# Values first by token tile in the first attention, and shared statistics for two norms in a row, in a two-stack transformer on one core

## The reference, cut to what matters

```
def first_block(x, ...):                       # layer 1 (second layer)
    k_blocks, v_blocks, k_mean = shared_kv(x, kv_norm, w_kv)   # rmsnorm(x, kv_norm) @ w_kv
    h = rmsnorm(x, norm_mixer[layer])
    q = (h @ w_q[j]).reshape(B, T, N_HEADS, HEAD_DIM)
    o = moba_attention(q, k_blocks, v_blocks, k_mean, rel_bias)
    x = x + o @ w_o[j]
    x = x + swiglu(rmsnorm(x, norm_ffn[layer]), w_gate_up[layer], w_down[layer])
    return rmsnorm(x, final_norm)              # = the second stack's x
rmsnorm(x, g) = x * rsqrt(mean(x*x) + 1e-6) * g
```

## Time and profile before

| | us |
|---|---|
| median of three runs | 1184.52 |
| profiled execution, its own time | 1182.94 |
| span of the profiled execution | 1180.9 |
| TensorE busy | 1142.3 (97%) |
| VectorE busy | 786.6 (67%) |
| ScalarE busy | 536.1 (45%) |
| GpSimd busy | 35.1 (3%) |

### The profile page before, as it was taken

The page is one execution under the profiler, slowest core; times in us unless marked ns, Lnnn a source line. Parts: engine busy times, 40 slices in busy tenths (PEclk is TensorE's granted clock), DMA queues, the critical chain, the costliest instruction groups (busy, mean ns, idle before and its releaser), DMA issues.

```text
span 1180.9 us, 17170 instructions
## 1 busy us (share of the span) xinstructions
PE 1142.3 (97%) x6750; PEld 992.2 (84%) x6750; DVE 786.6 (67%) x990; ACT 536.1 (45%) x696; POOL 35.1 (3%) x49
## 2 busy tenths in 40 slices
PE   6899999899999999998999999999999999999997
PEld 4788888799878888888988788888899887888886
DVE  4766666746667666666677676666766766766665
ACT  4534334446654334335566543343345665433432
POOL 0000000000000000001200000000030000000000
PEclk9899999999999999998999999999999999999999
DMA  9565656664337555575623375556763234665560
GB/s 286 186 213 183 206 181 201 195 210 140 114 115 231 187 191 194 197 214 155 198 76 105 116 236 187 191 191 199 214 179 117 94 108 143 198 194 181 183 205 36
DMA packets 167672, 205.14 MB, mean 174 GB/s; under 512 B 19983, under 2 KB 150535, under 8 KB 167618
## 3 DMA queue, kind: packets, MB, share of 16 engines
q1 hardware_dynamic: 167618, 204.40, 53.7%
HBM read 203.22 MB, written 1.16 MB: 173 GB/s over the span
## 4 chain that ended last, share of the span: by engine, by line
PE 91%; DVE 3%; SPq 2%; ACT 2%; issue 1%; POOL 1%; DMA 0%; DVEq 0%; POOLq 0%; ACTq 0%
PE bank L1296 27%; PE bank L1300 14%; PE bank L1270 13%; PE bank L1271 13%; PE bank L1272 13%; PE bank L1487 3%; PE bank L1499 2%; PE bank L1379 1%; ACT junk L626 1%; PE bank L1509 1%; POOL rstd L564 1%; PE bank L1701 1%; DVE xn L907 1%; DVE x L889 1%; PE bank L1644 1%
## 5 line engine op out<-in xcount | busy, mean ns | idle before, releaser
L615 ACT ACTIVATE whi<-raw 128x2048 fp32r<-128x2048 f32 x177 | 339.0, 1916 | 414.0 <-PE bank L1300 271.4
L879 DVE TENSOR_TENSOR wlo<-raw,whi 128x2048 fp32r<-128x2048 f32 x177 | 405.7, 2294 | 162.9 <-ACT whi L615 162.8
L1296 PE MATMUL bank<-h_both,whi 128*128 128x512 f32 x1376 | 327.6, 390 | 0.0
L1296 PEld LDWEIGHTS bank<-h_both,whi 128*128 128x128 f32 x1376 | 255.0, 188 | 50.8
L1300 PEld LDWEIGHTS bank<-h_both,wlo 128*128 128x128 f32 x1376 | 176.7, 191 | 6.9
L1300 PE MATMUL bank<-h_both,wlo 128*128 128x256 f32 x1376 | 178.8, 283 | 0.0
L1270 PE MATMUL bank<-whi,o_hi 128*128 128x512 f32 x448 | 176.0, 393 | 0.6 <-DVE o_lo L1088 0.6
L1271 PE MATMUL bank<-wlo,o_hi 128*128 128x512 f32 x448 | 174.9, 390 | 0.0
L1272 PE MATMUL bank<-whi,o_lo 128*128 128x512 f32 x448 | 174.4, 389 | 0.0
L1270 PEld LDWEIGHTS bank<-whi,o_hi 128*128 128x128 f32 x448 | 84.3, 188 | 18.4 <-issue 2.3
L1272 PEld LDWEIGHTS bank<-whi,o_lo 128*128 128x128 f32 x448 | 84.1, 188 | 18.0
(11 more groups left out here) (154 smaller groups left out, 1146.8 us busy)
## 6 DMA issues: line engine op xcount, KB each, us to landing
raw<-in_w_gate_up SPq DMA_DIRECT2D x44, 1024.0 KB, 5.0
raw<-in_w_down SPq DMA_DIRECT2D x44, 1024.0 KB, 4.8
raw<-in_w_gate SPq DMA_DIRECT2D x22, 1024.0 KB, 5.3
raw<-in_w_up SPq DMA_DIRECT2D x22, 1024.0 KB, 5.2
raw<-in_w_in SPq DMA_DIRECT2D x20, 1024.0 KB, 6.1
raw<-in_w_o SPq DMA_DIRECT2D x12, 1024.0 KB, 4.8
raw<-in_w_kv SPq DMA_DIRECT2D x8, 1024.0 KB, 5.5
raw<-in_w_q SPq DMA_DIRECT2D x4, 1024.0 KB, 5.8
```

Of the source, the lines that this page charges most:

```text
L615: act.activation(whi[:, s, :], raw[:, s, :], ACT.Copy).then_inc(hi_ready, 1)
L879: dve.tensor_tensor(wlo[:, s, :], raw[:, s, :], whi[:, s, :].bitcast(F32), ALU.subtract).then_inc(lo_ready, 1)
L1296: pe.matmul(bank[bk + jj][:, :], hi[:, kc, jj * P:(jj + 1) * P], h_both[:, kc, :, :].rearrange("p a t -> p (a t)"), start=(kc == 0), stop= ...
```

## The change

In the first attention, the norm for keys and values comes first (version 2, now into `h_hi` and `h_lo`), the one for queries second (version 3, into `o_hi` and `o_lo`). Unit 0 is the values of head group 0, token-major: `first_token_major` for tile 0, then the transposes of tile 1, then tile 1. Unit 1 is the keys of group 0, with the transposes of the query norm between its two passes. Units 2 to 5 are the query quarters, and unit 2 is the one that goes through `first_feature_major`. VectorE gets its own order for this norm (`kv_norm`), in which the low part of unit 1's weights is computed in two halves between the steps of the norm.

Between the stacks, ScalarE squares both `x` (into `ssq`) and `x` times the final norm's gain (into `usq`), which VectorE writes to `xn`. Both powers of a tile are taken in one GpSimd instruction over two columns. The mixers' input is the scaled `xn` times one scalar times the gain; the new residual `x` is formed afterwards (`residual_out`), that of tile 1 behind the split of unit 84.

```
 def moba_script():
-    s = [("q_norm",)]
...
-    s += unit(0) + [("kv_norm",)] + unit(1) + [("kv_h",)]
+    s = [("kv_h",), ("q_norm",)] + unit(0) + [("q_h",)] + unit(1)
...
         def moba_src(n):
-            if n < 4:
-                return k8(a["w_q"][0], 256 * n)
+            if n < 2:
+                return k8(a["w_kv"], 0 if n else D)
+            if n < 6:
+                return k8(a["w_q"][0], 256 * (n - 2))
...
 # GpSimd, between the stacks
             for t in range(TT):
-                for v in (4, 5):
-                    rsqrt_tile(v, t)
+                pool.wait_ge(msq_ready, tile_no(5, t) + 1)
+                pool.tensor_tensor(rstd[:, t:t + 7:6], msq[:, t:t + 7:6], neghalf[:, 0:2], ALU.pow).then_inc(rstd_ready, 2)
...
 # ScalarE, between the stacks
+                    for h in range(2):
+                        square_x(0, h)
+                        square_scaled(0, h)
+                    split(u0 + 1)
+                    square_x(1, 0)
+                    square_x(1, 1)
+                    h_out(6, 0, 0)
+                    h_out(6, 0, 1)
+                    square_scaled(1, 0)
+                    square_scaled(1, 1)
                     for h in range(2):
                         h_out(6, 1, h)
...
 # VectorE, first attention
+            def kv_norm():
+                add_residual(2, 0, 0)
+                add_residual(2, 0, 1)
+                mean_square(2, 0)
+                normalise(2, 0, 0)
+                normalise(2, 0, 1)
+                add_residual(2, 1, 0)
+                h_lo_out(2, 0, 0)
+                h_lo_out(2, 0, 1)
+                add_residual(2, 1, 1)
+                split_half(MOBA_U + 1, 0)
+                mean_square(2, 1)
+                normalise(2, 1, 0)
+                normalise(2, 1, 1)
+                split_half(MOBA_U + 1, 1)
+                h_lo_out(2, 1, 0)
+                h_lo_out(2, 1, 1)
...
 # VectorE, between the stacks (final_norm_1)
+                def scaled(t, h):
...
+                    dve.tensor_tensor(xn[:, t, cols], x[:, t, cols], gx[:, cols], ALU.mult).then_inc(scaled_ready, 1)
+                def mean_squares(t):
...
+                    dve.tensor_scalar(msq[:, t:t + 1], ssq[:, t, 0:1], ssq[:, t, 1:2], EPS, ALU.add, ALU.add).then_inc(msq_ready, 1)
...
+                    then_wait(dve.tensor_scalar(msq[:, 6 + t:7 + t], msq[:, t:t + 1], EPS, usq[:, t, 0:1], ALU.mult, ALU.add))
+                    dve.tensor_tensor(msq[:, 6 + t:7 + t], msq[:, 6 + t:7 + t], usq[:, t, 1:2], ALU.add).then_inc(msq_ready, 1)
...
+                for h in range(2):
+                    add_residual(4, 0, h)
+                    scaled(0, h)
+                mean_squares(0)
+                add_residual(4, 1, 0)
+                add_residual(4, 1, 1)
+                for h in range(2):
+                    mixer_input(0, h)
+                for h in range(2):
+                    scaled(1, h)
+                for h in range(2):
+                    h_lo_out(6, 0, h)
+                mean_squares(1)
+                residual_out(0, 0)
+                for h in range(2):
+                    mixer_input(1, h)
+                residual_out(0, 1)
                 for h in range(2):
                     h_lo_out(6, 1, h)
+                split(MIX_U[0] + 1)
+                for h in range(2):
+                    residual_out(1, h)
...
 # TensorE, first attention
+                    if n == 0:
+                        first_token_major(u, 4, 0, 2)
+                        transposes(2, 1)
+                        used(first_token_major(u, 4, 1, 2))
+                    elif n == 1:
+                        feature_major(u, 5, ALL, 0, H)
+                        for t in range(TT):
+                            transposes(3, t)
+                        used(feature_major(u, 5, ALL, 1, H))
+                    elif n == 2:
+                        pe.wait_ge(proj_out, 1)
+                        used(first_feature_major(u, 4, O, 3))
```

More of the change, by code:

```diff
@@ L734, in _ @@
                 k = ev[0]
[L735 removed]
+                if k == "kv_h":
                     norm(2, late_split=MOBA_U + 1)
[L737 removed]
+                elif k == "q_h":
                     norm(3, False)
@@ L768, in mix, with next_square, square_x, square_scaled @@
                 if l == 0:
[L769 to L778, removed]
+                    done = [16]
+                    def next_square(src, t, h, acc):
+                        act.wait_ge(squares, done[0])
+                        act.activation(junk[:, :], src[:, t, h * HALF:(h + 1) * HALF], ACT.Square, scale=1.0 / 32,
+                                       accum_out=acc[:, t, h:h + 1]).then_inc(squares, 1)
+                        done[0] += 1
+                    def square_x(t, h):
+                        act.wait_ge(x_ready, 12 + 2 * t + h + 1)
+                        if t == 0 and h == 0:
+                            act.wait_ge(msq_ready, tile_no(3, 1) + 1)
+                        next_square(x, t, h, ssq)
+                    def square_scaled(t, h):
+                        act.wait_ge(scaled_ready, 2 * t + h + 1)
+                        next_square(xn, t, h, usq)
+                    for h in range(2):
[8 more added lines that the diff above has]
+                    square_scaled(1, 1)
                     for h in range(2):
@@ L942, in norm, with split_half @@
                         h_lo_out(j, t, h)
+            def split_half(n, part):
+                s = slot_of(n)
+                cols = slice(part * UNIT // 2, (part + 1) * UNIT // 2)
+                if part == 0:
+                    dve.wait_ge(hi_ready, n + 1)
+                i = dve.tensor_tensor(wlo[:, s, cols], raw[:, s, cols], whi[:, s, cols].bitcast(F32), ALU.subtract)
+                if part:
+                    i.then_inc(lo_ready, 1)
+            def kv_norm():
[15 more added lines that the diff above has]
+                h_lo_out(2, 1, 1)
             def lambdas():
@@ L1116, in _ @@
                 k = ev[0]
[L1117 to L1120, removed]
+                if k == "kv_h":
+                    kv_norm()
+                elif k == "q_norm":
                     for t in range(TT):
@@ L1142, in final_norm_1 @@
             def final_norm_1():
[L1144 to L1155, removed]
+                gx, gz = gains[:, 1, :], gains[:, 0, :]
@@ new lines, in scaled @@
+                def scaled(t, h):
+                    cols = slice(h * HALF, (h + 1) * HALF)
+                    if (t, h) == (0, 0):
+                        dve.wait_ge(gains_in[1], 16 * 3)
+                        dve.wait_ge(xT_ready, 4 * (HT_NO[6] - 1))
+                    dve.wait_ge(x_ready, 12 + 2 * t + h + 1)
+                    dve.tensor_tensor(xn[:, t, cols], x[:, t, cols], gx[:, cols], ALU.mult).then_inc(scaled_ready, 1)
+                def mean_squares(t):
+                    dve.wait_ge(squares, 22 if t else 19)
+                    dve.wait_ge(rstd_ready, tile_no(4, t))
+                    dve.tensor_scalar(msq[:, t:t + 1], ssq[:, t, 0:1], ssq[:, t, 1:2], EPS, ALU.add, ALU.add).then_inc(msq_ready, 1)
+                    dve.wait_ge(msq_ready, tile_no(4, t) + 1)
+                    dve.wait_ge(squares, 16 + 4 * t + 4)
+                    then_wait(dve.tensor_scalar(msq[:, 6 + t:7 + t], msq[:, t:t + 1], EPS, usq[:, t, 0:1], ALU.mult, ALU.add))
+                    dve.tensor_tensor(msq[:, 6 + t:7 + t], msq[:, 6 + t:7 + t], usq[:, t, 1:2], ALU.add).then_inc(msq_ready, 1)
@@ new lines, in mixer_input, with residual_out @@
+                def mixer_input(t, h):
+                    cols = slice(h * HALF, (h + 1) * HALF)
+                    if (t, h) == (0, 0):
+                        dve.wait_ge(gains_in[0], 16 * 4)
+                    dve.wait_ge(rstd_ready, tile_no(5, t) + 1)
+                    dve.scalar_tensor_tensor(out=xn[:, t, cols], in0=xn[:, t, cols], scalar=rstd[:, 6 + t:7 + t],
+                                             in1=gz[:, cols], op0=ALU.mult, op1=ALU.mult).then_inc(xn_ready, 1)
+                def residual_out(t, h):
+                    cols = slice(h * HALF, (h + 1) * HALF)
+                    dve.scalar_tensor_tensor(out=x[:, t, cols], in0=x[:, t, cols], scalar=rstd[:, t:t + 1],
+                                             in1=gx[:, cols], op0=ALU.mult, op1=ALU.mult).then_inc(x_ready, 1)
@@ L1165, in mix @@
                     norm(8)
-                split(u0 + 1)
+                    split(u0 + 1)
                 for ev in mix_script():
@@ L1518, in _ @@
                 k = ev[0]
[L1519 to L1524, removed]
+                if k == "unit":
                     n = ev[1]
```

28 lines of the change are left out of this document (14 added, 14 removed).

## The result

The changed kernel took 1177.11 us, the median of four runs (1176.73 to 1178.07), against 1184.36 for the kernel before (1183.73 to 1184.72, four runs): 7.2 us less. The ratio is 0.9934, 95% interval [0.9919, 0.9949]; that times the 1184.52 shown ahead is 1176.7 us (1174.9 to 1178.5). The forecast was 1178.1: the sign is right, and the gain was put at 6.4 us for 7.2 by the medians, 7.8 by the ratio. The 1176.7 lies 0.1 us under the range, whose low end was 1176.8; the interval reaches over the forecast itself. The profiled execution of the changed kernel took 1178.07 with a span of 1176.0.

The account below looks back on a forecast made before the run. TensorE, working 97% of the span, was taken as the bound. Gains of 3.8 us in the first attention and 2.6 between the stacks, 6.4 in all, took 1184.52 to 1178.1 us, range 1176.8 to 1181.2.

Parts of the forecast that it names:

- Part A: First attention: with values and keys first, unit 1 starts at 230.37 in place of 234.20, 3.8 us earlier.
- Part B: Between the stacks: shared statistics start unit 84 at 543.59 in place of 546.17, 2.6 us earlier.
- the first rival: Between the stacks: the lower clock moves to unit 83's second pass or unit 84, losing 1.7 us: 1179.8 us; 20%.
- one of the prediction's own signs of being wrong: Between the stacks: the prediction is wrong if half clock lies on unit 83's second pass or unit 84.
- the sentence under the sum: Rest of the kernel: moves along unchanged, since TensorE is the bound everywhere in it and keeps its order.
- The bounds of A and B: Gain limits: first attention 2.1 to 4.2 us, between the stacks 0.9 to 3.1 us.
- the half clock that moves: Between the stacks: half clock moves to unit 83's second pass or unit 84 instead of going: 1179.8 us; 20%.
- B gives nothing: Between the stacks: ScalarE's squares, split and copies stand in one row, so no gain there: 1180.7 us; 10%.
- A half: First attention: half splits or a late query norm hold TensorE in unit 1, halving the gain: 1180.0 us; 7%.
- slower: Both changed starts: the clock stays low through them, two 6.8 us stretches at half clock giving 1184.9 us; 3%.

Follow-up runs that it names:

- e5: Kernel before, with unread matmuls filling TensorE's holes at the second to fourth feed-forward block, in the first attention and between the stacks: median 1181.30 us.
- e8: Kernel before with only the first attention's change, holes filled between the stacks and at the second to fourth feed-forward block: median 1179.31 us.
- e3: Kernel before with only the change between the stacks, first attention as before: median 1181.03 us, ratio 0.9961.
- e12: The changed kernel, nothing altered, one more single execution with its trace: 1176.72 us.
- e4: Changed kernel with five unread matmuls of 512 columns in each of TensorE's two holes between the stacks: median 1175.70 us.
- e10: The kernel before, nothing altered, one more single execution with its trace: 1183.96 us.
- e6: Changed kernel with unread matmuls filling the holes between the stacks and at the second to fourth feed-forward block: median 1174.97 us.
- e7: Filled changed kernel, residual_out(0, 0) behind tile 1's mixer inputs, residual_out(0, 1) behind unit 84's split, four matmuls for five in one hole: median 1174.94 us.

## Why the prediction was wrong in size and right in kind

- **Part A, 3.8 us: right.** Laying the third norm start over the first gave unit 1 at 230.37; it came at 230.80 in an execution that stood 0.46 late (223.00 against 222.54), so at 230.34. The half split costs what was worked out: the mean square stands 0.26 late (224.74 - 0.46 against 859.32 - 635.30 = 224.02), and the idle time is 0.58 for the 0.6 forecast. Of the 3.9, 2.6 are order and 1.3 half clock that the old order drew on itself (e5, e8): all seven traces with the old order unfilled have 3.4 us of it there, none of the others has any.
- **Part B, 2.6 us: the chain right, its clock not.** Tile 1's mixer input was forecast 11.90 behind the first residual and came at 11.55. Of that, 0.22 was there in the last small operation (10.14 for 10.36), because tile 0's mixer inputs and copies started that much sooner: I had put 0.24 us between the end of the last matmul and the residual, and there is next to nothing. From that operation to the mixer input it was 1.41 us for 1.54, with the power at 1.08 for 1.14. Part B is worth 2.9 us at full clock (e3, e12), 1.7 when half clock falls on unit 83's second pass, the first rival and one of the prediction's own signs of being wrong, seen in two of three traces of the changed kernel. The rival's price of 1.7 us for it was too high, it cost 1.2. The prediction also took the 4.5 us of unit 83's first pass before as a pass at the lower clock; half clock ended at 540.5, before its last eight matmuls. The sum does not rest on this.
- **The step that failed** is the sentence under the sum: what is left of the kernel "moves along unchanged". The forecast put this term at nothing. No instruction of it changed and TensorE kept its order, but a stage's length depends on where its start lies. From the mean of the four traces of the kernel before to that of the three of the changed one, 7.5 us in all: A 4.0, M1 2.1, F1 0.4, F2 1.6, start and F0 together 0.2, and F3 0.8 back. So the two places changed gave 6.2 us for the 6.4 forecast, and what was to move along unchanged gave 1.4 for nothing. I had read the half clock as a price paid at the two places changed; it is paid at the four feed-forward starts as well, and the change moved three of them. The starts of F2 and F3 show it, first before, then in e12:

```profile
660.00:676.00 16.00, 13.88 (x72) 11.31 (x71) 11.08 (x16) 9.42 (x15) 1.55 (x2) 0.89 0.22 67
980.00:995.00 15.00, 12.55 (x72) 10.12 (x71) 10.24 (x16) 9.68 (x15) 1.55 (x2) 1.00 0.22 71
```

```profile
660.00:672.00 12.00, 9.82 (x63) 8.31 (x64) 11.39 (x13) 6.29 (x10) 0.99 (x1) 1.00 0.18 57
974.00:989.00 15.00, 12.67 (x62) 10.78 (x61) 12.08 (x16) 9.27 (x15) 1.55 (x2) 0.77 0.24 70
```

- The 1.4 us are of few traces, and it was chance that they added up so. F2 had half clock in all four traces of before and in none of the changed kernel; F3 had it in two of four and in all three. And e4, the changed kernel but for two filled holes, has 6.8 us of it in F2 again (189.12). From e10 (1183.96) to e12 (1176.72) A gave 4.13 and M1 3.04, while F1 with 1.09, F2 with 0.98, start and F0 with 0.36 and F3 with 2.36 back nearly cancel. The bounds of A and B give 1177.2; the range's low end had 0.4 us on top of them, and no term for this.
- Of the rivals, the half clock that moves is shown; that B gives nothing, or A half, is refuted by the stages; slower is refuted by the times.
- One trace of before was too little: of some fifty other executions of this kernel only one was faster than its 1182.94.

## The best version

The changed kernel with its holes filled (e6): 1174.97 us, ratio to the kernel before 0.9908 [0.9892, 0.9925], 2.4 us under the changed kernel's 1177.39. The two come from different comparisons, but the highest run of e6 (1175.41) lies under the lowest of the changed kernel (1175.83). It costs some forty matmuls of no use and takes the spread from 3.8 to 1.2 us.

## What to carry to other kernels

A norm before a token-major unit need not stop TensorE: tile 0's pass covers tile 1's norm. Where a stretch of the same form already exists in the trace, lay it over the one to be changed; here it foretold the next unit's start to 0.1 us. But before a gain of a few us is summed, look at several executions and cut them into stages: half clock behind short holes comes and goes with the position, and a shift of 1.7 us gained elsewhere as much as it cost (1184.99 against 1185.05).

## What the runs showed of the hardware

- Half clock behind a norm start of this kernel came in stretches of 3.4 or 6.8 us. In a feed-forward block they cost 1.1 and 2.3 us (186.82, 187.9, 189.1). Between the stacks it came behind two holes of 1.4 us with transposes and one pass between them, and the same start had it in one execution and not in another. The Trainium skill (TensorE: Matmul & The Clock Gate, Part 1: The HAM clock gate) calls the number of slow matmuls at a kernel's start run-variable; in the middle of this kernel it varies too, M1 being 134.19 or 135.44 long for one kernel.
- A GpSimd power of two columns took 0.70 us with VectorE idle (e7) and beside a VectorE addition that reads PSUM (at 527.51), and 1.08 beside a VectorE instruction with two inputs in SBUF.
- A float32 product of two SBUF tiles of 512 columns took VectorE 0.69 us, the same as an addition that reads PSUM.
